# Compressed attention branch of a hybrid decoder layer: keys stationary in column quarters, one transpose for a group of heads

## The reference

```python
def compress_kv(kv, w1, w2, pos_emb):
    ...
    blocks = jnp.concatenate([chunks[:, :, i:i + n_cmp] for i in range(n_sub)], axis=3) + pos_emb
    return jax.nn.gelu(blocks.reshape(B, G, n_cmp, CMP_BLOCK * d) @ w1) @ w2
...
    logits = jnp.einsum('bgrsd,bgnd->bgrsn', q, kc) * ATTN_SCALE + head_bias(rel_table, dist_c)
    p_cmp = masked_softmax(logits, dist_c >= 0)
    o_cmp = jnp.einsum('bgrsn,bgnd->bgrsd', p_cmp, vc)
```

## Time and profile before

| what | us |
|---|---|
| median of 3 runs | 1048.48 |
| lowest, highest | 1047.56, 1048.55 |
| profiled execution | 1049.22 |
| its span | 1047.50 |
| PE busy in the span | 930.3 (89%) |
| DVE busy | 731.6 (70%) |
| ACT busy | 294.1 (28%) |
| POOL busy | 332.7 (32%) |

### The profile page before, as it was taken

How to read it: one execution, slowest core, us unless ns; L and a number is a source line. 1 busy time by engine, 2 the same in 40 slices (tenths; PEclk the granted TensorE clock), 3 DMA queues, 4 the chain that set the end, 5 groups by cost and what they waited for, 6 DMA issues and landing times.

```text
span 1047.5 us, 11317 instructions
## 1 busy us (share of the span) xinstructions
PE 930.3 (89%) x3445; PEld 563.9 (54%) x3445; DVE 731.6 (70%) x1933; ACT 294.1 (28%) x802; POOL 332.7 (32%) x324
## 2 busy tenths in 40 slices
PE   8999999999999999899999968868686877886886
PEld 6788888888746684565566423323232332332332
DVE  6599799664565177966867866867777677677454
ACT  4211122264465122432232221212312212212223
POOL 0100102011000025354443754445444454454420
PEclk9999999999999999999999998998989899899889
DMA  9966947897103859999999999999999999999994
GB/s 360 402 258 192 373 160 283 327 334 143 61 21 137 326 194 422 409 376 423 421 421 421 422 423 423 421 423 424 422 423 425 421 423 424 421 423 422 423 423 173
DMA packets 63147, 361.93 MB, mean 346 GB/s; under 512 B 7484, under 2 KB 8140, under 8 KB 30062
## 3 DMA queue, kind: packets, MB, share of 16 engines
q0 software_dynamic: 43136, 292.59, 68.5%
q1 hardware_dynamic: 19950, 68.61, 17.7%
HBM read 359.58 MB, written 1.59 MB: 345 GB/s over the span
## 4 chain that ended last, share of the span: by engine, by line
PE 54%; DMA 33%; DVE 6%; ACT 2%; SPq 2%; issue 2%; POOL 1%; ACTq 0%; POOLq 0%; DVEq 0%
DMA arena<-in_peer_uv,idx 21%; PE pb L556 20%; PE pb L801 18%; DMA ring<-in_peer_uv,idx 11%; PE pb L781 3%; PE pb L729 2%; PE pb L739 2%; PE pb L830 2%; DMA arena<-in_w_ada 2%; DVE arena L1484 2%; PE pb L679 2%; PE pb L591 1%; PE pb L702 1%; POOL arena L519 1%; ACT sig L1076 1%
## 5 line engine op out<-in xcount | busy, mean ns | idle before, releaser
L801 PE MATMUL pb<-arena,sig 128*128 128x512 f32 x416 | 197.7, 628 | 27.0 <-ACT sig L1076 27.0
L556 PE MATMUL pb<-hT,ring 128*128 128x256 f32 x752 | 162.8, 379 | 0.5 <-ACT arena L906 0.5
L801 PE MATMUL pb<-ring,sig 128*128 128x512 f32 x288 | 138.0, 623 | 25.9 <-ACT sig L1076 25.9
L519 POOL DMA_INDIRECT arena<-in_peer_uv,idx x104 | 122.4, 1177 | 121.2 <-PE pb L801 95.6
L801 PEld LDWEIGHTS pb<-arena,sig 128*128 128x128 f32 x416 | 82.5, 201 | 136.2 <-issue 136.1
L1484 DVE CUSTOM_DVE_ANT_0 arena<-arena,sig 128x1024 f32<-128x1024 f32 x104 | 124.4, 1224 | 44.4 <-DMA arena<-in_peer_uv,idx 43.9
L556 PEld LDWEIGHTS pb<-hT,ring 128*128 128x128 f32 x752 | 142.7, 190 | 21.1 <-ACT arena L906 1.7
L1073 ACT ACTIVATE gl<-dot 128x4 f32<-128x4 f32 (+1 forms) x73 | 14.9, 205 | 383.6 <-DVE dot L1484 359.0
L519 POOL DMA_INDIRECT ring<-in_peer_uv,idx x72 | 86.9, 1207 | 87.2 <-PE pb L801 79.6
L801 PEld LDWEIGHTS pb<-ring,sig 128*128 128x128 f32 x288 | 56.5, 201 | 102.4 <-issue 102.2
L1484 DVE CUSTOM_DVE_ANT_0 ring<-ring,sig 128x1024 f32<-128x1024 f32 x72 | 87.6, 1224 | 34.2 <-DMA ring<-in_peer_uv,idx 33.7
(11 more groups left out here) (313 smaller groups left out, 1229.9 us busy)
## 6 DMA issues: line engine op xcount, KB each, us to landing
ring<-in_w_stream SPq DMA_DIRECT2D x79, 512.0 KB, 7.0
arena<-in_w_ada POOLq DMA_DIRECT2D x32, 512.0 KB, 10.8
arena<-in_w_ada SPq DMA_DIRECT2D x12, 512.0 KB, 11.8
arena<-in_w_stream SPq DMA_DIRECT2D x8, 512.0 KB, 6.7
arena<-in_w1k SPq DMA_DIRECT2D x6, 512.0 KB, 8.6
more<-in_w_stream SPq DMA_DIRECT2D x5, 512.0 KB, 13.3
sig<-in_w_ada SPq DMA_DIRECT2D x4, 512.0 KB, 14.8
more<-in_w1v POOLq DMA_DIRECT2D x1, 2048.0 KB, 18.1
```

The source lines that it names most:

```text
L519: nc.gpsimd.indirect_dma_start(out=rowat[PLACE[n]], out_offset=None, in_=a["peer_uv"], in_offset=bass.IndirectOffsetOnAxis(ap=idx[:, c, e: ...
L556: last = mm(pb[:, bank, 0:SEQ], w[:, k * P:(k + 1) * P], src[:, k, :], start=(k == 0), stop=(k == DT - 1))
L801: last = mm(pb[:, 4 + 2 * t + hf, :], diag[:, c % DEEP, e, :], rowat[PLACE[n]][:, D + hf * 512:D + (hf + 1) * 512], start=(i == 0 and e == ...
```

## The change

- The compressed scores swap operands: the compressed keys of the group (32 columns, of which the last 17 yield rows that nothing uses) are stationary and 128 query positions stream. Each head of the group writes its own 32 partitions of one PSUM bank, that is its own quarter of the array's columns (`cmp_scores`, now at the end of the group before). The result has keys on partitions. ACT copies it to SBUF (`cmp_scores_out`, `scT`), and one PE transpose turns it back to tokens on partitions (`cmp_scores_turned`). DVE reads it from there as before.
- `Sc` becomes a view of `Scp`, in which each head has 32 columns, the last 17 of them zero. `cmp_transposes` turns all four heads in one transpose of 128 columns, and ACT's copy takes 128 columns instead of 512.
- The compressed values get a padded form `vc4` with 128 rows for each head, zero outside the head's 15. So the value product takes all 128 partitions, with one matmul for each head. For this the second layer of the values is computed four times, into the four quarters (32 matmuls instead of 8), and copied by four ACT instructions. It now stands after the wait for `kcT` and ahead of the first `cmp_scores`.
- In units 3, 6, 8, 11 and 14, where a new column of the convolution begins, `conv_pieces` goes behind the unit's transposes.
- POOL clears the three padded tiles at the program's start.

The diff, with context left out:

```diff
@@ -256,7 +256,7 @@
...
         spare = sb("spare", [P, 2 * D])
-        PcT = spare[:, 1024:2048].rearrange("p (u t) -> p u t", u=2)
+        PcT = spare[:, 1024:1280].rearrange("p (u t) -> p u t", u=2)
         htok = spare[:, 0:256].rearrange("p (u n) -> p u n", u=2)
@@ -288,9 +288,11 @@
...
         hidv = left[:, 128:256].rearrange("p (h c) -> p h c", h=2)
-        kcT = sb("kcT", [DQK, NCG])
-        vcv = left[0:NCMP, 256:256 + GROUPS * DV]
-        Sc = sb("Sc", [P, REP, NCMP])
+        kcT = sb("kcT", [DQK, 80])
+        scT = left[:, 256:384]
+        vc4 = more[:, 4, :].rearrange("p (g h d) -> p g h d", g=GROUPS, h=REP)
+        Scp = sb("Scp", [P, REP, 32])
+        Sc = Scp[:, :, 0:NCMP]
         nmc = sb("nmc", [P, REP])
@@ -373,6 +375,7 @@
...
         v_h2T = sem("v_h2T")
+        p_cqk, a_cqk = sem("p_cqk"), sem("a_cqk")
 
@@ -456,6 +459,9 @@
...
             nc.gpsimd.memset(tbc[:, 0, :, NFAR:NCMP], NEG).then_inc(g_rowok, 1)
+            nc.gpsimd.memset(Scp[:, :, :], 0.0).then_inc(g_rowok, 1)
+            nc.gpsimd.memset(kcT[:, NCG:80], 0.0).then_inc(g_rowok, 1)
+            nc.gpsimd.memset(vc4[:, :, :, :], 0.0).then_inc(g_rowok, 1)
             g_ch.link(nc.gpsimd.memset(rowok[:, :], 1.0))
@@ -642,14 +648,6 @@
...
             last.then_inc(p_kc, 1)
-            pe.wait_ge(a_hv, 1)
-            for g in range(GROUPS):
-                for k in range(2):
-                    last = mm(pb[0:NCMP, 5, 256 + g * DV:256 + (g + 1) * DV], hidv[:, k, g * NBLK:g * NBLK + NCMP],
-                              w2v[:, k, :], start=(k == 0), stop=(k == 1))
-            last.then_inc(p_vc, 1)
-
-
             pe.wait_ge(a_kc, 1)
@@ -658,19 +656,21 @@
...
                 for hh in range(REP):
-                    last = mm(pb[:, 6 + (gi + 1) % 2, hh * NCMP:(hh + 1) * NCMP], qT[0:DQK, g * REP + hh, tt * P:(tt + 1) * P],
-                              kcT[:, g * NBLK:g * NBLK + NCMP], start=True, stop=True)
-                last.then_inc(p_cs, 1)
+                    last = mm(pb[hh * 32:(hh + 1) * 32, 6 + (gi + 1) % 2, 0:P], kcT[:, g * NBLK:g * NBLK + 32],
+                              qT[0:DQK, g * REP + hh, tt * P:(tt + 1) * P], start=True, stop=True)
+                last.then_inc(p_cqk, 1)
+
+            def cmp_scores_turned(gi):
+                pe.wait_ge(a_cqk, gi + 1)
+                nc.tensor.transpose(pb[:, 6 + (gi + 1) % 2, P:2 * P], scT, ident[:, :]).then_inc(p_cs, 1)
 
...
                 else:
-                    pe.wait_ge(a_vc, 1)
-                for hh in range(REP):
-                    last = nc.tensor.transpose(pb[0:NCMP, 5, hh * P:(hh + 1) * P], Sc[:, hh, :], ident[:, :])
-                last.then_inc(p_ct, 1)
+                    pe.wait_ge(a_vc, REP)
+                nc.tensor.transpose(pb[:, 5, 0:P], Scp[:, :, :].rearrange("p h n -> p (h n)"), ident[:, :]).then_inc(p_ct, 1)
 
@@ -696,11 +696,12 @@
...
 
-                def sides(v, table, first, final):
+                def sides(v, table, final):
 
...
                         last = mm(pb[odd * DV:(odd + 1) * DV, 6 + gi % 2, 0:2 * P].rearrange("p (a t) -> p a t", t=P), v,
-                                  table.rearrange("k (a b t) -> k a b t", b=2, t=P)[:, :, odd, :], start=first, stop=final)
+                                  table.rearrange("k (a b t) -> k a b t", b=2, t=P)[:, :, odd, :], start=False, stop=final,
+                                  skip_group_check=True)
                     return last
@@ -708,13 +709,15 @@
...
                     pe.wait_ge(v_cs, min(gi + 2, GROUPS * TT))
-                    sides(vcv[:, g * DV:(g + 1) * DV], PcT[0:NCMP, gi % 2, :], True, False)
+                    for hh in range(REP):
+                        mm(pb[hh % 2 * DV:(hh % 2 + 1) * DV, 6 + gi % 2, hh // 2 * P:(hh // 2 + 1) * P], vc4[:, g, hh, :],
+                           PcT[:, gi % 2, :], start=(hh < 2), stop=False, skip_group_check=True)
                 pe.wait_ge(a_pt, REP * (gi + 1))
...
                     last = sides(V[:, kb, (b * GROUPS + g) * DV:(b * GROUPS + g + 1) * DV],
-                                 PT[:, gi % 2, b * (tt + 1) + kb, :], False, (b, kb) == products[-1])
+                                 PT[:, gi % 2, b * (tt + 1) + kb, :], (b, kb) == products[-1])
                     if (b, kb) == products[-1]:
@@ -741,18 +744,32 @@
...
 
+            pe.wait_ge(a_hv, 1)
+            for g in range(GROUPS):
+                for k in range(2):
+                    for hh in range(REP):
+                        last = mm(pb[hh * 32:hh * 32 + NCMP, 5, 256 + g * DV:256 + (g + 1) * DV],
+                                  hidv[:, k, g * NBLK:g * NBLK + NCMP], w2v[:, k, :], start=(k == 0), stop=(k == 1))
+            last.then_inc(p_vc, 1)
+            cmp_scores(0)
             for n in range(NU + 2):
+                fresh = n < len(CO_UNITS) and 0 in CO_UNITS[n][1] and n > 0
                 if n < NU:
-                    if n % REP == 0:
-                        cmp_scores(n // REP)
                     scores(n)
-                conv_pieces(n)
+                if not fresh:
+                    conv_pieces(n)
                 if n >= 2:
                     transposes(n - 2)
+                if n < NU and n % REP == 0:
+                    cmp_scores_turned(n // REP)
+                if fresh:
+                    conv_pieces(n)
                 if n < NU and n % REP == 2:
...
                     values((n - REP - 2) // REP, (n - REP - 2) % REP)
+                if n % REP == REP - 1 and n < NU - 1:
+                    cmp_scores(n // REP + 1)
                 if n == NU:
@@ -962,12 +979,21 @@
...
             act.wait_ge(p_tv, 1)
-            fn(hidv[:, :, 0:NCG], pb[:, 5, 0:P].rearrange("p (a b) -> p a b", a=2)[:, :, 0:NCG],
-               ACT.Copy).then_inc(a_hv, 1)
+            fn(hidv[:, :, :], pb[:, 5, 0:P].rearrange("p (a b) -> p a b", a=2), ACT.Copy).then_inc(a_hv, 1)
             act.wait_ge(p_kc, 1)
-            fn(kcT[:, :], pb[0:DQK, 6, 256:256 + NCG], ACT.Copy).then_inc(a_kc, 1)
+            act.wait_ge(g_rowok, 5)
+            fn(kcT[:, 0:NCG], pb[0:DQK, 6, 256:256 + NCG], ACT.Copy).then_inc(a_kc, 1)
+            def cmp_scores_out(gi):
+                act.wait_ge(p_cqk, gi + 1)
+                act.wait_ge(p_cs, gi)
+                fn(scT, pb[:, 6 + (gi + 1) % 2, 0:P], ACT.Copy).then_inc(a_cqk, 1)
+
+            cmp_scores_out(0)
             act.wait_ge(p_vc, 1)
-            fn(vcv[:, :], pb[0:NCMP, 5, 256:256 + GROUPS * DV], ACT.Copy).then_inc(a_vc, 1)
+            for hh in range(REP):
+                fn(vc4[hh * 32:hh * 32 + NCMP, :, hh, :],
+                   pb[hh * 32:hh * 32 + NCMP, 5, 256:256 + GROUPS * DV].rearrange("p (g d) -> p g d", g=GROUPS),
+                   ACT.Copy).then_inc(a_vc, 1)
 
@@ -999,13 +1025,15 @@
...
                         fn(Sc[:, :, :], Sc[:, :, :], ACT.Exp, scale=SCALE).then_inc(a_cexp, 1)
+                if n % REP == REP - 1 and n < NU - 1:
+                    cmp_scores_out(gi + 1)
                 if n >= 2:
...
                         act.wait_ge(p_o, gi - 1)
-                    fn(PcT[0:NCMP, gi % 2, :], pb[0:NCMP, 5, :], ACT.Copy).then_inc(a_pct, 1)
+                    fn(PcT[:, gi % 2, :], pb[:, 5, 0:P], ACT.Copy).then_inc(a_pct, 1)
                 if n >= 2 * REP + 2 and n % REP == 2:
@@ -1251,7 +1279,7 @@
...
             dve.wait_ge(a_v, 6)
-            dve.wait_ge(g_rowok, 2)
+            dve.wait_ge(g_rowok, 5)
             ch.add(V_.tensor_scalar(gates[:, 0, 0, :], gates[:, 0, 0, :], rowok[:, :], None, ALU.mult))
@@ -1279,7 +1307,7 @@
...
                     dve.wait_ge(p_ct, gi)
-                V_.tensor_tensor(Sc[:, :, :], pb[:, 6 + (gi + 1) % 2, 0:REP * NCMP].rearrange("p (h n) -> p h n", h=REP),
+                V_.tensor_tensor(Sc[:, :, :], pb[:, 6 + (gi + 1) % 2, P:2 * P].rearrange("p (h n) -> p h n", h=REP)[:, :, 0:NCMP],
                                  tbc[:, tt, g * REP:(g + 1) * REP, :], ALU.add).then_inc(v_cs, 1)
```

## The result

| | before | after |
|---|---|---|
| median, us (5 runs each) | 1048.35 | 1042.01 |
| lowest, highest | 1047.11, 1048.55 | 1041.46, 1042.51 |
| ratio, 95% interval | | 0.9942 (0.993 to 0.9955) |
| profiled execution, its span | 1049.22, 1047.5 | 1042.01, 1040.3 |

The changed kernel is 6.3 us faster; the interval of the ratio is 4.7 to 7.3 us.

A forecast was written before the change was run, and what follows sets the result against it. Attention units, PE busy 82.71 of 87.17 us, were taken to move the gathers and the end one for one. Terms +1.0 - 3.18 - 2.24 + 0.22 - 0.09 + 0.0 = -4.3 us gave 1044.2; range 1042.6 to 1047.9.

The forecast's parts named there:

- group 0: First four units (one head of one 128-token tile each): ACT's first exponential 2.9 us after first score, DVE 0.8 late.
- rounds of four at L615's round price: L751, the compressed values' second layer: 64 passes as 16 rounds at 0.122, 1.95 us, costing +0.95.
- The halves rival: L751 and L659: quarters overlap no deeper than halves, L751 3.9, L659 0.64; net -0.3 us, 1048.1; chance 0.17.
- the signs that the prediction named: L751 near 1.95, L659 near 0.4, unit 4's score 1.0 later, unit 16's 1.2 earlier, first L732 and gathers 4.3 earlier.
- the 0.4 allowed for scatter of the runs: Low end of the range: 0.4 us taken off the all-cheap case of 1043.0, giving 1042.6.
- paid in full (+0.9): First units: ACT's late start costs its whole delay without cover, +1.9 instead of +1.0; part of the rival Gain lost.
- L673's saving: Transpose of the group's probabilities: four transposes become one, -0.32 us a group, -2.24 for groups 1 to 7.
- the added transpose: L665, turning scores back: 0.11 us on PE each, covered in the second tile, +0.22 in groups 2 and 3.
- the pieces behind transposes: Conv pieces at units 6 and 14: transposes fill PE's wait for DVE, 2 x -0.21 = -0.42 us.
- one after the other: Rival at L751 and every L659: quarters run serially, net +2.7 us, 1051.2; chance 0.07.
- Gain lost: Rival: ACT's late start, DVE waits leave the stage 2 us or less, or gathers start no earlier; about 1047; chance 0.11.
- Deeper than charged: Rival at L751 and the start: L751 takes 1.0 and the lag is covered, -5.5 us, 1043.0; chance 0.10.

The follow-up runs named there:

- Experiment 6: Changed kernel with all four heads' L751 and L659 matmuls in one column quarter (1050.25 us, ratio 1.0011), then in two (1045.06 us, measured once); results partly overwritten.
- Experiment 7: Changed kernel with ACT's four copies of the values moved behind the exponentials of unit 1: 1042.12 us, measured once.
- experiment 2: Kernel before with only the new scores, their ACT copy and the transpose back; values, probabilities and conv pieces as before: 1044.92 us, ratio 0.997.
- experiment 4: Changed kernel with every conv piece ahead of its unit's transposes again: 1043.08 us, ratio 0.9963.
- experiment 9: Changed kernel with L751 ahead of the kcT wait, ACT's value copies behind unit 1's exponentials, transpose back right behind each group's first score: 1040.81 us, ratio 0.9915.
- the clearing alone: Kernel before with two of the three padded tiles and their POOL memsets, nothing else of the change: 1048.46 us, ratio 1.0007.
- swap alone: The run of experiment 2, the kernel before with only the scores' operands swapped: 1044.92 us, ratio 0.997.
- old scores: Changed kernel with the old form of the group's scores (queries stationary, no ACT copy, no transpose back): 1045.24 us, ratio 0.9975.
- conv first: The run of experiment 4, the changed kernel with conv pieces ahead of the transposes: 1043.08 us, ratio 0.9963.
- the changed kernel again: The run of experiment 5, the changed kernel repeated without edits: 1042.86 us, ratio 0.9933.
- one quarter: The first run of Experiment 6, the changed kernel with L751 and L659 sent to a single column quarter: 1050.25 us, ratio 1.0011.
- best: The kernel of experiment 9, the changed kernel with three moves: 1040.81 us, ratio 0.9915.
- experiment 5: The changed kernel run again without edits, beside the kernel before on chip 14: 1042.86 us, ratio 0.9933.

## Why the prediction missed

| term | predicted | measured |
|---|---|---|
| start (L649 to first score) | +0.83 | -0.29 |
| group 0 | +0.17 | +0.64 |
| groups 1 to 7 | -5.29 | -5.53 |
| values(7), behind the stage | no term | -0.14 |
| sum | -4.3 | -5.32 |

**The step that failed** is "I take rounds of four at L615's round price, 16 x 0.122 = 1.95" for L751. L751 measured 0.90. The mechanism was right, quarters overlap. The size was wrong: L615 streams 128 columns a pass and L751 only 64, so its pass is half as long. The right row was L648's own pace, 0.0625 a pass, which the text had as its lower bound: 16 x 0.0625 = 1.0. Experiment 6 shows 0.056 in each of three arrangements. The halves rival has the same slip: it priced L751 at 3.9, and in two quarters it took 1.80, less than the forecast had for four. Of the signs that the prediction named, only L659 near 0.4 came as said. Counted from the keys' layer, unit 4's scores were 0.35 later and not 1.0, unit 16's 2.13 earlier and not 1.2, the first attention output 5.18 earlier and not 4.3.

That term explains the miss at the start, not the miss of the range. A stage and values(7) of -5.32 would have put the median at 1043.2, inside it. What carries the result out of the range is the last microsecond (see below), and the term that failed there is the 0.4 allowed for scatter of the runs. The medians of the same changed kernel alone are 1042.01 and 1042.86.

Groups 1 to 7 gave 0.24 more than forecast, from small terms. L659, taken at 0.39, measured 0.36 in six groups, some 0.15 in all: its passes stream 128 columns as L615's do, but four side by side cost 0.107 a round (experiment 6) and not L615's 0.122. L713 with a first-tile group took 0.59, not 0.49 and 0.15; with a second-tile group it and the V product behind it took 0.14 less than before, not 0.09. Against that, L673 saves 0.33 in the first tile and 0.28 in the second, not 0.32, and a part of the second tile's gain goes into waits for DVE.

The Trainium skill (TensorEngine Tiling, Instruction Overhead) has about 60 cycles for each matmul however small, an estimated 1.6 us for 64 passes one behind the other. The trace says 0.90, 0.014 a pass, so read as a floor for the whole engine the page does not hold for passes that alternate between quarters. The Trainium skill (TensorE: Matmul & The Clock Gate, Part 3, Measured speedup vs the span model) has one matmul plus about 4 ns for each further tile. The prediction's 0.36 for L659 left the 4 ns out; with three further tiles in each of two rounds it is an estimated 0.39. The trace has 0.33 to 0.36, and in L751 the 16 rounds would have had an estimated 0.19 us of it over 16 x 0.056 = 0.90; it shows none. So the trace agrees with the one matmul, and L751 shows nothing of the 4 ns.

**Group 0** was charged with too little. The prediction had ACT's first exponential 2.9 us after the first score and DVE 0.8 late for unit 3, mostly made up by PE's shorter work (+0.17). The exponential came at 3.18, as each of the four copies took 0.4 and not 0.3, and group 0 cost 0.64, although it holds the 0.22 of the third conv place that nobody had counted. Experiment 7 gets 0.89 back by moving the copies. The rival had "paid in full (+0.9)" as its price, so the mechanism was named and put on the wrong side. Start and group 0 together: +1.0 forecast, +0.35 measured, two errors of opposite sign.

**Right:** L673's saving to 0.04 a group; the added transpose hidden in the second tile and 0.11 in groups 2 and 3 (experiment 2: 0.42 there, 0.53 in groups 4 to 6); the 0.33 by which DVE is late for unit 6 (5.49 against 5.16 in experiments 2 and 4 and in the changed kernel), of which experiment 9 moves 0.20; a switch of shape saved before V products; the gathers moved with the stage (from the first attention output to the 7th gather 59.21 us, 59.36 before, of which 0.14 is values(7)). **Half right:** the pieces behind transposes. Two places were counted at 0.21; experiment 4 has 0.22 at three.

**The rivals.** Halves, and one after the other: refuted by the 0.90 and 0.33 of the changed kernel, and by experiment 6. Gain lost: refuted as a whole, since the stage gives 5.18; its +0.9 for ACT was right. Deeper than charged (-5.5, 1043.0) was the nearest, for half its reason: L751 was short, the lag was not covered.

**The last microsecond.** The stage and values(7) give 5.32, the first medians 6.34. Median against before, less the same sum from the traces: the clearing alone +0.48, swap alone +0.28, old scores -0.03, conv first -0.22 on chip 1; the changed kernel again -0.82, one quarter -1.16, best -1.18 on chip 14. What is left over goes for the most part with the set of runs and the kernel before in it (medians 1048.35, 1047.97 and 1048.99). Within chip 1 there is also half a microsecond between the two kernels that keep the old values and the two that don't, no more than these medians scatter. Where the scatter can lie, the traces show: L649 started anywhere between 240.04 and 242.81 us, and the 7th gather to the end spread over 1.1. So I put the rest down to scatter of the two edges; that the interval of the ratio, 4.7 to 7.3 us, holds 5.32 fits. No run isolates it, so its cause is argued and not shown. The range had allowed 0.4 us for this, less than the 1.0 by which medians of the kernel before differ. Of the 2.2 us between forecast and result 1.0 is mis-sized terms, 0.1 the median of before, and 1.0 this rest.

## What to carry to other kernels

- Price a tiled matmul by the passes in its fullest tile and by its own streamed columns; take the pace from a row with the same streamed length, not from the row with the same layout.
- When work on one engine becomes cheap through replication (here four copies of a small product), look at who copies the copies out: PE got the fourfold layer for next to nothing (1.02 us against 1.00, each with full-width work behind it), ACT paid 1.2 us more for it, just ahead of the first exponential, and moving its copies took 0.9 off the stage. Such copies belong behind the first use of the engine that everybody waits for.
- A piece of work put ahead of a wait that another engine sets saves its own length, once for each place where the wait really stands (0.22 a place for 0.21 of transposes).

## What was not expected of the hardware

- Replicating a product into four column quarters was free on PE: 64 passes with 64 streamed columns take 0.90 us in four quarters, 1.80 in two, 3.58 in one, and 1.02 in four with full-width work behind them; the 16 passes of the old form took 1.00.
- For a stationary operand of 32 columns and 128 streamed, two passes a quarter take 0.33 to 0.36 us in all; of that 0.11 to 0.15 does not depend on the number of passes.
- Four ACT copies of 15 x 256 from four partition quarters take 1.6 us, 0.4 each, as long as one of the copies alone (0.37): small copies do not overlap on ACT.
- In the attention units, where DMA is 0.20 to 0.24 busy and no engine waits for a transfer, equal code repeats to 0.01 us over 84 us, and single groups do so between chip 1 and chip 14 (groups 2 and 4 to 7 of experiments 4 and 5). What scatters lies outside: 2.8 us ahead of L649, and 1.1 behind the 7th gather.
